# Expert matrices of nine of sixteen pairs loaded whole, in two transfers of 64 partitions, in a decoder layer with 32 experts

## The reference, cut to what matters

```python
def moe(h, w_router, b_router, w_gate, b_gate, w_up, b_up, w_down, b_down):
    t = h.reshape(B * T, D)
    logits = (t @ w_router + b_router).astype(jnp.float32)
    top_v, top_i = lax.top_k(logits, TOP_K)
    probs = jax.nn.softmax(top_v, axis=-1)
    comb = jnp.sum(jax.nn.one_hot(top_i, N_EXPERTS, dtype=jnp.float32) * probs[..., None], axis=1)
    y = jnp.zeros((B * T, D), jnp.float32)
    for e in range(N_EXPERTS):
        gate = jnp.minimum(t @ w_gate[e] + b_gate[e], SWIGLU_LIMIT)
        up = jnp.clip(t @ w_up[e] + b_up[e], -SWIGLU_LIMIT, SWIGLU_LIMIT)
        hid = (up + 1.0) * gate * jax.nn.sigmoid(gate * SWIGLU_ALPHA)
        y = y + comb[:, e:e + 1] * (hid @ w_down[e] + b_down[e]).astype(jnp.float32)
```

## Time and profile before

| | |
|---|---|
| median of 3 runs | 1334.15 us (1333.44 to 1334.32) |
| profiled execution | 1333.15 us |
| its span, from the first to the last instruction | 1331.4 us |
| mean granted TensorE clock | 0.997 |
| TensorE (PE) busy | 1276.5 us, 96% |
| VectorE (DVE), ScalarE (ACT), GpSimd (POOL) busy | 30%, 14%, 1% |
| moved by DMA | 464.25 MB |
| of it by the queue that SP issues to (q1) | 459.53 MB, 83.2% of 16 engines |

### The profile page before, as it was taken

One profiled execution on the slowest core, in us unless ns is written; L12 is line 12 of the kernel. 1 busy time (PEld: TensorE's weight loads), 2 busy tenths in 40 slices (PEclk: granted clock), 3 DMA queues, 4 the chain that ended last, 5 costly groups with the idle time before them and its releaser, 6 DMA issues.

```text
span 1331.4 us, 18885 instructions
## 1 busy us (share of the span) xinstructions
PE 1276.5 (96%) x8184; PEld 635.4 (48%) x8184; DVE 405.4 (30%) x820; ACT 190.4 (14%) x351; POOL 16.1 (1%) x39
## 2 busy tenths in 40 slices
PE   7999999999999999999999999999999999999995
PEld 5777865677784434434344333433333343443332
DVE  3998624532122121221312213112121311212122
ACT  3015222321221000100001000010100000010002
POOL 0002000000000000000000000000000000000000
PEclk9999999999999999999999999999999999999998
DMA  7335131285997999999999999999999999999995
GB/s 251 135 112 133 54 129 64 100 350 198 415 367 313 429 414 427 428 428 427 429 429 427 428 429 428 429 428 428 430 428 429 428 428 429 429 428 428 428 426 206
DMA packets 40280, 464.25 MB, mean 349 GB/s; under 512 B 8528, under 2 KB 10128, under 8 KB 12064
## 3 DMA queue, kind: packets, MB, share of 16 engines
q1 hardware_dynamic: 39392, 459.53, 83.2%
q0 software_dynamic: 832, 3.90, 0.9%
HBM read 458.34 MB, written 5.07 MB: 348 GB/s over the span
## 4 chain that ended last, share of the span: by engine, by line
PE 64%; DMA 26%; DVE 7%; ACT 1%; issue 0%; SPq 0%; DVEq 0%
PE ps L1109 32%; PE ps L567 20%; DMA arena<-in_w_gate 13%; DMA ring<-in_w_gate 10%; PE ps L1177 4%; DVE arena L1499 4%; DMA ring<-in_w_down 2%; PE ps L1133 2%; PE ps L1120 2%; DVE ring L1496 1%; PE ps L1126 1%; PE ps L1211 1%; PE ps L1167 1%; DVE arena L1496 1%; PE ps L1138 1%; DVE ring L1499 1%
## 5 line engine op out<-in xcount | busy, mean ns | idle before, releaser
L1109 PE MATMUL ps<-ring,xT 128*64 128x512 f32 x1536 | 342.7, 596 | 8.3 <-DMA ring<-in_w_up 5.5
L567 PE MATMUL ps<-arena,ring 128*128 128x288 f32 (+2 forms) x1152 | 231.4, 371 | 0.0
L1109 PEld LDWEIGHTS ps<-ring,xT 128*64 128x64 f32 x1536 | 105.9, 137 | 235.1 <-issue 208.4
L567 PEld LDWEIGHTS ps<-arena,ring 128*128 128x128 f32 (+1 forms) x1152 | 179.4, 176 | 45.8 <-issue 4.5
L1109 PE MATMUL ps<-ring,arena 128*64 128x512 f32 x768 | 171.7, 596 | 10.0 <-DMA ring<-in_w_down 10.0
L1253 ACT ACTIVATE arena<-ps 128x512 f32<-128x512 f32 (+5 forms) x136 | 76.3, 569 | 599.3 <-PE ps L1126 330.8
L1109 PE MATMUL ps<-arena,xT 128*64 128x512 f32 x512 | 115.5, 595 | 3.1 <-DMA arena<-in_w_gate 3.1
L1109 PEld LDWEIGHTS ps<-ring,arena 128*64 128x64 f32 x768 | 53.2, 137 | 111.2 <-issue 97.4
L1921 DVE TENSOR_SCALAR xT<-ps 128x512 f32<-128x512 f32 x32 | 22.1, 692 | 185.3 <-PE ps L1109 185.3
L1109 PEld LDWEIGHTS ps<-arena,xT 128*64 128x64 f32 x512 | 35.6, 137 | 74.3 <-issue 66.8
L1876 DVE TENSOR_TENSOR xT<-ps,vec 128x1024 f32<-128x1024 f32 x15 | 18.4, 1225 | 171.6 <-PE ps L1138 171.6
(11 more groups left out here) (218 smaller groups left out, 791.9 us busy)
## 6 DMA issues: line engine op xcount, KB each, us to landing
ring<-in_w_up SPq DMA_DIRECT2D x64, 2048.0 KB, 31.9
ring<-in_w_down SPq DMA_DIRECT2D x47, 2048.0 KB, 31.5
ring<-in_w_gate SPq DMA_DIRECT2D x32, 2048.0 KB, 34.2
arena<-in_w_gate SPq DMA_DIRECT2D x32, 2048.0 KB, 34.3
arena<-in_w_down SPq DMA_DIRECT2D x16, 2048.0 KB, 34.8
ring<-in_w_in SPq DMA_DIRECT2D x4, 2048.0 KB, 12.1
ring<-in_cache_k SPq DMA_DIRECT2D x4, 2048.0 KB, 17.8
ring<-in_cache_v SPq DMA_DIRECT2D x4, 2048.0 KB, 8.7
```

Of the source, the lines that this page charges most:

```text
L567: return nc.tensor.matmul(out, lhsT, rhs, start=start, stop=stop)
L1109: last = nc.tensor.matmul(out[AT[h ^ swap], :], lhs(k), part(weights(i), 0, 4, D)[:, k % 4, h * 512:(h + 1) * 512], start=(fresh and k == ...
```

## The change

In pairs 6 to 14 (the seventh to the fifteenth) a matrix is loaded whole: SP waits until both of its slots are empty, and then issues two transfers, one for partitions 0 to 63 and one for 64 to 127, with a run of 32 KB in each partition. The first adds to `slot_in` of the slot of half 0, the second to that of half 1. TensorE waits for both ahead of k = 0, since each row block needs all partitions. Pairs 0 to 5 and pair 15 go on in halves of 128 partitions. In HBM a matrix is now one block of 128 rows of 32 KB, so the source rows of a half lie 32 KB apart where they lay 16 KB apart. The loop over pairs becomes two loops on SP and TensorE, with bounds at `WHOLE = 3`; the other engines keep theirs.

```diff
--- before.py
+++ after.py
@@ -8,6 +8,7 @@
 
 
 
+import functools
 from contextlib import ExitStack
 
 import concourse.bass as bass
@@ -35,6 +36,7 @@
 PICKED = PAIRS + 2
 TURNED = PAIRS + 1
 SLOTS = 8
+WHOLE = 3
 RING = 6
 RW = 14
 CT = 4
@@ -160,6 +162,10 @@
         def weights(i):
 
             return ring[:, i * SLOT:(i + 1) * SLOT] if i < RING else arena[:, (i - RING) * SLOT:(i - RING + 1) * SLOT]
+
+        def whole_slot(i):
+
+            return ring[:, i * SLOT:(i + 2) * SLOT] if i < RING else arena[:, 0:2 * SLOT]
 
         def C(name):
             at, n = CONST[name]
@@ -409,6 +415,20 @@
                 for dst, name in ((b_gate, "b_gate"), (b_up, "b_up"), (b_down, "b_down")):
                     sp.dma_start(dst, A[name]).then_inc(S["ext_ld"], 16)
 
+            def experts_whole(q, s, u, odd):
+                for n, (w, p) in enumerate(MATRICES):
+                    matrix = w[bass.ds(2 * q + p, 1), :, :].rearrange("a p f -> p (a f)")
+                    i, _ = place(odd, n, 1)
+                    done, val = emptied(odd, n, 1)
+                    if done == "slot_free":
+                        sp.wait_ge(slot_free[i], u * FREED[i] + val)
+                    else:
+                        sp.wait_ge(S[done], 2 * s + val)
+                    first_i, _ = place(odd, n, 0)
+                    for c in range(2):
+                        rows = slice(64 * c, 64 * (c + 1))
+                        sp.dma_start(whole_slot(first_i)[rows], matrix[rows]).then_inc(slot_in[place(odd, n, c)[0]], 16)
+
             def experts(q, s, u, odd, first=False, last=False):
                 for n, (w, p) in enumerate(MATRICES):
                     for c in range(2):
@@ -424,7 +444,7 @@
                                 sp.wait_ge(S[done], 2 * s + val)
                         if first and i == RING:
                             small()
-                        src = w[bass.ds(2 * q + p, 1), c, :, :].rearrange("a p f -> p (a f)")
+                        src = w[bass.ds(2 * q + p, 1), :, c * SLOT:(c + 1) * SLOT].rearrange("a p f -> p (a f)")
                         if last and (n, c) == (5, 1):
                             for k in range(4):
                                 sp.dma_start(weights(i)[:, k * D:(k + 1) * D], src[:, k * D:(k + 1) * D]).then_inc(S[f"piece{k}"] if k < 3 else slot_in[i], 16)
@@ -441,10 +461,13 @@
 
             experts(0, 0, 0, 0, first=True)
             experts(1, 1, 0, 1)
-            with sp.Fori(1, PAIRS // 2 - 1) as t:
+            with sp.Fori(1, WHOLE) as t:
                 for odd in range(2):
                     experts(2 * t + odd, 2 * t + odd, t, odd)
-            experts(PAIRS - 2, PAIRS - 2, PAIRS // 2 - 1, 0)
+            with sp.Fori(WHOLE, PAIRS // 2 - 1) as t:
+                for odd in range(2):
+                    experts_whole(2 * t + odd, 2 * t + odd, t, odd)
+            experts_whole(PAIRS - 2, PAIRS - 2, PAIRS // 2 - 1, 0)
             experts(PAIRS - 1, PAIRS - 1, PAIRS // 2 - 1, 1, last=True)
             results(0)
             sp.wait_ge(S["route_ready"], 1)
@@ -464,14 +487,19 @@
             sp.wait_ge(S["conv_sent"], 16 * 9)
             sp.wait_ge(S["state_sent"], 16)
 
-        def rounds(eng, step, closing, next_round=None):
+        def rounds(eng, step, closing, next_round=None, whole=None):
 
             step(0, 0, 0, 0, 0, first=True)
             step(0, 1, 1, 0, 1)
-            with eng.Fori(1, PAIRS // 2 - 1) as t:
+            later = whole or step
+            with eng.Fori(1, WHOLE if whole else PAIRS // 2 - 1) as t:
                 for odd in range(2):
                     step(0, 2 * t + odd, 2 * t + odd, t, odd)
-            step(0, PAIRS - 2, PAIRS - 2, PAIRS // 2 - 1, 0)
+            if whole:
+                with eng.Fori(WHOLE, PAIRS // 2 - 1) as t:
+                    for odd in range(2):
+                        whole(0, 2 * t + odd, 2 * t + odd, t, odd)
+            later(0, PAIRS - 2, PAIRS - 2, PAIRS // 2 - 1, 0)
             step(0, PAIRS - 1, PAIRS - 1, PAIRS // 2 - 1, 1, last=True)
             closing(0)
             eng.wait_ge(S["route_ready"], 1)
@@ -1097,10 +1125,13 @@
             nc.tensor.matmul(ranks[:, 2, :], before32, mask[:, 2, :], start=False, stop=True, skip_group_check=True).then_inc(S["pos_ps"], 1)
             AT = (slice(0, CAP), slice(CAP, P))
 
-            def multiply(out, lhs, n, u, odd, ks, fresh, done=None, swap=False, r=0, pieces=False):
+            def product(out, lhs, n, u, odd, ks, fresh, done=None, swap=False, r=0, pieces=False, both=False):
 
                 for k in ks:
                     i, fill = place(odd, n, k // 4)
+                    if both and k == 0:
+                        i1, fill1 = place(odd, n, 1)
+                        pe.wait_ge(slot_in[i1], u * 48 + 16 * (fill1 + 1 + FRONT_FILLS[i1]))
                     if pieces and 4 <= k < 7:
                         pe.wait_ge(S[f"piece{k - 4}"], r * 16 + (32 if k == 4 else 16))
                     elif k == 0 or k == 4 or pieces and k == 7:
@@ -1180,7 +1211,10 @@
                                                     start=False, stop=True, skip_group_check=True)
                         last.then_inc(S["scat_done"], 1)
 
-            def step(r, q, s, u, odd, first=False, last=False):
+            def step(r, q, s, u, odd, first=False, last=False, both=False):
+                def multiply(*args, **kinds):
+                    product(*args, both=both, **kinds)
+
                 def in_xe(p):
                     return lambda k: xe[:, k, p, :]
 
@@ -1242,7 +1276,7 @@
                     last = nc.tensor.matmul(psG[TAIL * d:TAIL * (d + 1), 0:1], lane32, ssq[:, 2:3], start=True, stop=True)
                 last.then_inc(S["tail_ps"], 1)
 
-            rounds(pe, step, closing, next_round)
+            rounds(pe, step, closing, next_round, functools.partial(step, both=True))
 
         @block.scalar
         def _(act):
@@ -2005,7 +2039,7 @@
 
     def quarters(w):
 
-        return w.reshape(NE, 2, 4, P, D).transpose(0, 1, 3, 2, 4).reshape(NE, 2, P, 4 * D)
+        return w.reshape(NE, KT, P, D).transpose(0, 2, 1, 3).reshape(NE, P, KT * D)
 
     xT = np.concatenate([a["x_prompt"][0], a["x_sample"].reshape(-1, D)]).T.reshape(KT, P, TOK).transpose(1, 0, 2)
     w_in = a["w_in"][0].reshape(KT, P, -1, P)
```

## The result

The changed kernel takes 1878.55 us (median of 4 runs, 1875.6 to 1882.32), the kernel before 1333.8 in the same series: a ratio of 1.4087, with a 95% interval of 1.4064 to 1.411. It is 544.7 us slower. The profiled execution took 1877.91 us, with a span of 1876.0.

What follows compares the result with a forecast made beforehand. The weight stream was taken to bound the kernel from the seventh pair on; half-partition loads at about 220 GB/s add 501 us to 1333.15, the other terms adding nothing: 1834 us, range 1328 to 1940.

Steps and rivals of the forecast that it cites:

- The bound: From the seventh pair on the weight stream sets the end one for one, 58.72 us a pair at 428.6 GB/s.
- Step (6): Loads in the nine changed pairs: transfers to 64 partitions run at about 220 GB/s, 114.4 us a pair, 501 us more.
- Step (5): Weight loads in nine pairs: runs double, packets halve; 432 fewer per engine at 12 ns, 5.2 us, taken as 4 us gain.
- Steps (1) and (2): TensorE waits for both transfers, SP for both slots; the queue's depth covers it, cost 0, else up to 3.65 us once.
- Step (3): Weight source rows in HBM lie 32 KB apart in the other seven pairs as well; cost 0.
- step (4): A second loop body on TensorE and SP, one more loop entry; cost 0.
- R1: In the changed pairs' stream the two halves overlap and only the packet gain is left: 1329 us; 20%.
- R2: Halves overlap, but 32 KB runs still move as two packets, or late slots eat the packet gain: 1333 us; 8%.
- R4: The whole-matrix wait starves the load queue, up to 3.65 us a matrix, 197 us, 1530 us; 2%.
- R3: Changed pairs' transfers overlap partly, between 264 and 425 GB/s; at 320 GB/s 179 us more, 1512 us; 10%.
- The clock: In the changed pairs, TensorE's work at half clock, 110 us of a pair's 114.4, would stay under the loads.
- idle over half of the time: Sign expected in the changed pairs: TensorE idle over half of the time on loads of matrices.

Runs made afterwards that it cites:

- e1: The change, but each whole matrix comes in one transfer of 128 partitions with 32 KB runs; 1330.89 us, 0.9973 of the kernel before.
- e2: The change, but the two transfers of a matrix take the even and the odd partitions, not the lower and upper 64; 1330.67 us, 0.9974 of the kernel before.
- e6: The change, but each whole matrix comes in four transfers of 32 adjacent partitions with 32 KB runs; 1878.02 us.
- e7: The change, but each partition's 32 KB come as two 16 KB runs, from the HBM layout of the kernel before; 1880.96 us.
- e8: The kernel before, with its transfers of halves in runs of 8 KB instead of 16 KB; 1346.46 us, 1.0101 of the kernel before.
- e3: The change with its waits and second loop, but the two transfers are halves of 128 partitions with 16 KB runs; 1336.47 us, 1.0016 of the kernel before.
- e4: Only the change's HBM layout against the kernel before, all pairs loaded in halves, no second loop; 1332.82 us, 0.9986 of the kernel before.
- e5: The change, but once, in the seventh pair's first matrix, four added transfers of 8 partitions put half the DMA engines one transfer out of step; 1892.62 us.

## Why the prediction was right, and where its terms were off

**The bound.** That the weight stream sets the end from the seventh pair on, one for one, held: 118.9 us a pair at 211.7 GB/s, with the DMA engines' share at 1.00.

**Step (6), half coverage.** The mechanism was right and decided everything. It was read from seven small loads that lasted six microseconds in all, and e1, e2, e6 and e7 show that it is which partitions a transfer covers, not how many, nor the length of the runs or the waits. What lies behind it in the hardware no trace shows. Its size was off: I took 220 GB/s, about midway between the lowest and the highest of the six rows (180 and 264; their mean is 233), and the steady rate is 211.7. Per pair that is 118.9 instead of 114.4 us, in nine pairs 9 x 4.5 = 40 us, and with it the forecast of 501 becomes 541 of the 544.7 measured. Part of the difference may be the edges of the event: its first and last rows are 264 and 262, the four between have a mean of 218, and full-width packets moved beside the partial ones. Half of the full rate (214) would have been the better choice, and it was in sight. That 64 partitions would do as 32 do was a guess, and e6 bears it out. A slip in the range changes nothing: with 264 GB/s the sum gives 1663 us, not 1675.

**Step (5), the packet gain.** 12 ns a packet was too much: e8 gives 8.8 to 9.5 ns, and 432 x 9.1 is 3.9 us. In e1, where the gain can be seen, the weights between 250 and 10 MB before the end of the stream take 556.5 us against 560.4 before, 3.9 less. By the windows the stream goes from 429 to 432 GB/s, which is 226.5 MB / 0.4286 - 226.5 / 0.432 = 4.2 us in the nine pairs, the 4 us that I took and not the 5.2 of the line. In the change itself it gains nothing visible.

**Steps (1) and (2), the waits, put at 0.** This was off by a little: e3, with the second loop, is 3.65 us slower than e4, which equals the most that I had named (3.65 us once, if the depth were gone) by chance, since the depth wasn't gone. The cover that I named, the depth of the queue, hides a late slot in the middle of the stream, but TensorE carries the lag into the sixteenth pair, and the last loads are issued late there. In the change itself the last 2 MB take 7.1 us against 6.1 before, so some 1 us of the 544.7 is lost there. In e1 and e2 they take 7.1 and 7.2, so there the waits cost about 1 us of the packet gain.

**Step (3), the layout, and step (4), the second loop.** E4 puts the layout at -1 us (0.9977 to 0.9994), so 0 was near. The loop wasn't tried alone; it is part of e3's 3.65 us, so it costs no more than a few microseconds.

**The rivals.** R1, that two halves in flight together would overlap, is refuted for this stream: over 1000 us of it no slice rises above 213, and with eight engines 0.8 of a transfer behind the other eight it stayed at 211 (e5). R2 falls by the count of packets and R4 by e3. R3 was not seen: the rate drops at once, within the window of 720 to 740 us, and stays.

**The clock.** I had noted that TensorE's work would fit even at half clock (110 us in 114.4). It did fall to the lower level in places, and the room, 118.9 us, was enough. One sign came out otherwise by it: I had expected TensorE to be idle over half of the time, and it was idle 43% of 800 to 1700 us (busy 511.40 us of 900), since part of its work ran at the lower clock.

## What to carry to other kernels

When a load is split by partitions, each part should still be spread over all 128: every second partition in one transfer and the rest in the next ran at the full rate here, while the lower and the upper half cost half of it, with six or seven transfers in flight. Look at the busy share of the DMA engines together with the rate: engines at 9 tenths and half the GB/s, as here, point to the shape of the transfers and not to too few of them. And a small event of that kind in the trace is worth reading: here six microseconds of it gave 233 GB/s, and the whole stream 212.

## What the runs showed of the hardware that was not expected

- A block of 32 adjacent partitions streams as fast as one of 64: 212 GB/s in both (e6 and the change).
- 64 partitions in steps of two stream at 432 GB/s (e2), no slower than all 128 in one transfer (e1, 432).
- The penalty is the same for packets of 16 KB (211 GB/s, e7) and of 32 KB (212), and putting eight of the engines 0.8 of a transfer behind the other eight doesn't lift it (211, e5).
- A DMA packet costs some 9 ns beyond its bytes (8.8 by e8's time, 9.1 and 9.5 by the amounts moved in e1 and e8), less than the 12 ns that the mean durations in the records suggest.
